# A mixture-of-experts layer whose experts are ranked on the chip, with fixed row counts per rank and column-tiled up-projections

## The reference

```
grp = argmax(x @ group_w + b)                    # top-1 of 4 groups
top2 = the two largest of the 8 expert logits in that group
gate = softmax(top2 logits) * softmax(group logits)[grp]
for each of 32 experts e, over the rows routed to it:
    h = silu(xb @ w1[e]) * (xb @ w3[e])          # 1024 -> 512, twice
    y += gate * (h @ w2[e])                      # 512 -> 1024
```

## Time and profile before

| | |
|---|---|
| median of 3 runs | 1710.05 us (1709.49 to 1710.27) |
| the profiled execution | 1708.72 us, of which the span is 1707.1 |
| TensorE busy | 1592.7 us, 93% |
| VectorE, ScalarE, GpSimd busy | 537.5, 396.1, 167.6 us |
| up-matmuls (L1703) | x1088, 480.1 us |
| down-matmuls (L1727) | x544, 240.9 us |
| the chain that ended last | TensorE 91% of the span |
| HBM read, written | 301.42 MB, 66.06 MB |

### The profile page before, as it was taken

How to read it: one execution, slowest core, us unless ns; L and a number is a source line. 1 busy time by engine, 2 the same in 40 slices (tenths; PEclk the granted TensorE clock), 3 DMA queues, 4 the chain that set the end, 5 groups by cost and what they waited for, 6 DMA issues and landing times.

```text
span 1707.1 us, 20384 instructions
## 1 busy us (share of the span) xinstructions
PE 1592.7 (93%) x7532; PEld 795.0 (47%) x7532; DVE 537.5 (31%) x1115; ACT 396.1 (23%) x578; POOL 167.6 (10%) x230
## 2 busy tenths in 40 slices
PE   7999999999999988998948999999999999999990
PEld 3444455546545545554524444444444444444440
DVE  4840064345536426353572111111111111111114
ACT  4020154354355343123411000000000000000004
POOL 2010000000000000100011111111011111111100
PEclk9999999999999998999967999999999999999995
DMA  5132132142132333335938788888889988898848
GB/s 216 50 113 74 66 130 80 45 142 88 50 104 77 112 136 127 135 119 198 336 125 356 263 336 336 332 332 334 336 339 344 343 332 333 332 332 334 332 157 307
DMA packets 76851, 368.43 MB, mean 216 GB/s; under 512 B 9072, under 2 KB 21872, under 8 KB 63600
## 3 DMA queue, kind: packets, MB, share of 16 engines
q1 hardware_dynamic: 57488, 300.90, 46.0%
q0 software_dynamic: 18720, 65.02, 12.4%
q10 hardware_dynamic: 576, 1.59, 0.2%
HBM read 301.42 MB, written 66.06 MB: 215 GB/s over the span
## 4 chain that ended last, share of the span: by engine, by line
PE 91%; DVE 3%; DMA 2%; issue 2%; ACT 2%; DVEq 0%; ACTq 0%; SPq 0%; POOLq 0%
PE bank L1703 28%; PE bank L1441 24%; PE bank L1727 14%; PE bank L1572 7%; PE bank L1453 5%; PE bank L1614 2%; PE bank L1696 2%; PE bank L1531 2%; PE bank L1548 1%; PE bank L1547 1%; PE bank L1526 1%; PE bank L1718 1%; PE bank L1632 1%; PE bank L1626 1%; PE bank L1483 1%
## 5 line engine op out<-in xcount | busy, mean ns | idle before, releaser
L1703 PE MATMUL bank<-wup,xgT 128*128 128x512 f32 x1088 | 480.1, 594 | 1.4 <-ACT xgT L935 1.4
L1441 PE MATMUL bank<-wide,mid 128*128 128x512 f32 x960 | 417.4, 594 | 2.6 <-issue 2.6
L1703 PEld LDWEIGHTS bank<-wup,xgT 128*128 128x128 f32 x1088 | 204.5, 191 | 246.2 <-issue 244.1
L1441 PEld LDWEIGHTS bank<-wide,mid 128*128 128x128 f32 x960 | 182.0, 191 | 227.7 <-issue 227.5
L1727 PE MATMUL bank<-wide,hidT 128*128 128x512 f32 x544 | 240.9, 596 | 4.2 <-DVE hidT L1411 4.2
L1727 PEld LDWEIGHTS bank<-wide,hidT 128*128 128x128 f32 x544 | 101.3, 191 | 119.3 <-issue 119.3
L1572 PE MATMUL bank<-early,mid 128*128 128x512 f32 x288 | 124.8, 592 | 0.0
L942 ACT ACTIVATE sil<-bank 128x512 f32<-128x512 f32 x34 | 20.3, 597 | 434.5 <-PE bank L1703 434.5
L1384 DVE TENSOR_SCALAR mid<-bank,gate_of 128x512 f32<-128x512 f32 x68 | 51.0, 751 | 212.3 <-PE bank L1727 212.3
L731 POOL DMA_INDIRECT x_dram<-mid,sidx x34 | 53.6, 1577 | 644.0 <-DVE mid L1384 297.3
L935 ACT ACTIVATE xgT<-bank 128x512 f32<-128x512 f32 x70 | 38.1, 594 | 275.1 <-PE bank L1696 275.1
(11 more groups left out here) (214 smaller groups left out, 1327.3 us busy)
## 6 DMA issues: line engine op xcount, KB each, us to landing
wup<-w SPq DMA_DIRECT2D x68, 2048.0 KB, 17.9
wide<-w SPq DMA_DIRECT2D x34, 2048.0 KB, 9.5
u_dram<-ustage POOLq DMA_DIRECT2D x60, 256.0 KB, 2.4
rin<-u_dram SPq DMA_DIRECT2D x60, 256.0 KB, 4.3
mid<-w_in SPq DMA_DIRECT2D x23, 512.0 KB, 3.4
wide<-x_t SPq DMA_DIRECT2D x12, 512.0 KB, 11.3
mix_dram<-mixst POOLq DMA_DIRECT2D x24, 256.0 KB, 2.6
mid<-x_all SPq DMA_DIRECT2D x12, 512.0 KB, 5.5
```

What stands on the lines that cost most here:

```text
L1441: last = pe.matmul(PROJ[u % 3][:, :], wsec[:, slot, k, :], nT[:, k, g * GT:(g + 1) * GT], start=(k == 0), stop=(k == KT - 1))
L1703: last = pe.matmul(bank[out_bank][:, :], xgT[:, k, :], weights[:, s, k, :], start=(k == 0), stop=(k == KT - 1))
```

## The change

Experts are ranked by their count, ties by number. Rank r has block r, whose number of rows is fixed: 128 for ranks 0 to 3, 112 for 4 to 15, 104 for 16 to 31. What an expert has beyond its capacity goes to extra blocks from number 32 on, up to 32 of them. The up products are turned round: 32 columns of the weights are the stationary operand in each of four column tiles, and the transposed rows move past them, so an instruction moves 104, 112 or 128 columns and not 512. The hidden values then come out transposed, and `transpose_hidden` and `copy_hidT` go; `hidT` has two buffers. [...] The count product of TensorE gives its result by expert and tile, so that one scan makes the running sums.

```diff
+CAPACITY = ((0, 128), (4, 112), (16, 104))
+MAIN_BLOCKS = NE
+MAX_OVER = -(-(2 * T // (CAPACITY[-1][1] + 1)) // EIGHT) * EIGHT
+BLOCK_COLUMNS = MAIN_BLOCKS + MAX_OVER + 2
@@ blocks_loop
-            pairs = (MIN_BLOCKS - first) // 2
-            with eng.Fori(0, pairs) as i:
-                for j in range(2):
-                    body(2 * i + (first + j), (first + j) % 2)
-            rest = first + 2 * pairs
-            with eng.Fori(0, -(-(MAX_BLOCKS - rest) // EIGHT)) as k:
+            if first % 2:
+                body(first, first % 2)
+                first += 1
+            ends = [b for b, rows in CAPACITY if b > first] + [MAIN_BLOCKS]
+            for start, end in zip([first] + ends[:-1], ends):
+                with eng.Fori(0, (end - start) // 2) as i:
+                    for j in range(2):
+                        body(2 * i + (start + j), (start + j) % 2, capacity(start))
+            rest = MAIN_BLOCKS
+            with eng.Fori(0, MAX_OVER // EIGHT) as k:
                 with eng.If(k * EIGHT + rest < used):
                     with eng.Fori(0, EIGHT // 2) as i:
                         for j in range(2):
                             with eng.If(k * EIGHT + 2 * i + (rest + j) < used):
...
@@ routing, VectorE
-            link(dve.memset(offset[:, 0, :], 0.0))
-            for t in range(NT):
-                link(dve.tensor_tensor(offset[:, t + 1, :], totals[:, t, :], offset[:, t, :], ALU.add))
+            link(dve.tensor_tensor_scan(upto[:, :, :].rearrange("p e t -> p (e t)"),
+                                        first_tile[:, :, :].rearrange("p e t -> p (e t)"),
+                                        bank[1][:, 0:NT * NE], 0.0, ALU.mult, ALU.add))
+            link(dve.tensor_tensor(above[:, :, :], counted[:, :].unsqueeze(1).to_broadcast([P, NE, NE]),
+                                   counted[:, :].unsqueeze(2).to_broadcast([P, NE, NE]), ALU.is_gt))
+            link(dve.tensor_reduce(rank[:, :], above[:, :, :], axis=AX.X, op=ALU.add))
...
+            link(dve.tensor_tensor(masked[:, :, :], slots[:, :, :], by_expert(cap), ALU.is_ge))
+            link(dve.tensor_tensor(masked[:, :, :], masked[:, :, :], by_expert(to_over), ALU.mult))
...
@@ blocks, VectorE
+                dve.tensor_tensor(hidT[:, s, :, :].rearrange("p k c -> p (k c)"), sil[:, :], bank[3][:, :],
+                                  ALU.mult).then_inc(hid_ready, 1)
@@ blocks, GpSimd
-            blocks_loop(pool, 3, used, rows_in_and_out)
+            for b in range(3, MAIN_BLOCKS):
+                rows_in_and_out(b, b % 2)
...
@@ blocks, TensorE
-                for k in range(KT):
-                    last = pe.matmul(bank[out_bank][:, :], xgT[:, k, :], weights[:, s, k, :],
-                                     start=(k == 0), stop=(k == KT - 1))
+                for f in range(FT):
+                    for k in range(KT):
+                        for c0 in range(0, P, SUB):
+                            last = pe.matmul(bank[out_bank][c0:c0 + SUB, f * P:f * P + rows],
+                                             weights[:, s, k, f * P + c0:f * P + c0 + SUB], xgT[:, k, 0:rows],
+                                             start=(k == 0), stop=(k == KT - 1), tile_position=(0, c0))
...
-            def expert_step(b, s):
-                first_up(b, s)
-                transpose_hidden(b - 1)
-                second_up(b, s)
+            def expert_step(b, s, rows=P):
+                first_up(b, s, rows)
+                second_up(b, s, rows)
                 transpose_rows(b + 1, 1 - s)
                 down(b - 1, 1 - s)
```

More of the change, by code:

```diff
@@ L53, with capacity @@
 FT = FE // P
-MAX_BLOCKS = (2 * T + NE * (P - 1)) // P
-MIN_BLOCKS = 2 * T // P
+CAPACITY = ((0, 128), (4, 112), (16, 104))
+MAIN_BLOCKS = NE
 EIGHT = 8
-BLOCK_COLUMNS = MAX_BLOCKS + 2
+MAX_OVER = -(-(2 * T // (CAPACITY[-1][1] + 1)) // EIGHT) * EIGHT
+BLOCK_COLUMNS = MAIN_BLOCKS + MAX_OVER + 2
+def capacity(b):
+    if not isinstance(b, int) or b >= MAIN_BLOCKS:
+        return P
+    return [rows for first, rows in CAPACITY if first <= b][-1]
 C_MIX, C_SCALE, C_GAIN, C_LB = 0, KT, KT + POOLS, KT + POOLS + 1
@@ L435, in blocks_loop @@
                             with eng.If(k * EIGHT + 2 * i + (rest + j) < used):
-                                body(k * EIGHT + 2 * i + (rest + j), (first + j) % 2)
+                                body(k * EIGHT + 2 * i + (rest + j), (rest + j) % 2)
         block = always.enter_context(nc.Block())
@@ L560, in _, with load_expert @@
             sp.wait_ge(blocks_known, 1)
-            used = sp.value_load(blocks_over[0:1, 0:1], min_val=0, max_val=MAX_BLOCKS - MIN_BLOCKS) + MIN_BLOCKS
-            def load_expert(b, s):
+            used = sp.value_load(blocks_over[0:1, 0:1], min_val=0, max_val=MAX_OVER) + MAIN_BLOCKS
+            def load_expert(b, s, rows=P):
+                first = isinstance(b, int) and b < 2
                 e = sp.value_load(expert_of[0:1, ds(b, 1)], min_val=0, max_val=NE - 1)
-                if not isinstance(b, int):
+                if not first:
                     sp.wait_ge(h1_ready, b - 1)
@@ L702, in _ @@
                       allow_small_or_imprecise_dtypes=True)
-            pool.affine_select(out=before[:, :], in_=ones[:, :], compare_op=ALU.is_gt, fill=0.0,
-                               base=0, pattern=[[1, P]], channel_multiplier=-1).then_inc(ranks_ready, 1)
+            pool.iota(expert_id[:, :], pattern=[[1, NE]], base=0, channel_multiplier=0,
+                      allow_small_or_imprecise_dtypes=True)
+            pool.memset(before[:, :], -1.0).then_inc(before_filled, 1)
+            pool.memset(first_tile[:, :, :], 1.0).then_inc(before_filled, 1)
+            pool.wait_ge(before_filled, 2)
+            pool.memset(first_tile[:, :, 0:1], 0.0)
+            pool.affine_select(out=before[:, :], in_=before[:, :], compare_op=ALU.is_ge, fill=0.0,
+                               base=0, pattern=[[-1, P]], channel_multiplier=1).then_inc(ranks_ready, 1)
             pool.wait_ge(parts_ready, 1)
@@ L744, in rows_in_and_out @@
                 add_outputs(b - 1, 1 - s)
-            blocks_loop(pool, 3, used, rows_in_and_out)
+            for b in range(3, MAIN_BLOCKS):
+                rows_in_and_out(b, b % 2)
+            with pool.Fori(0, MAX_OVER // EIGHT) as k:
+                with pool.If(k * EIGHT + MAIN_BLOCKS < used):
+                    with pool.Fori(0, EIGHT // 2) as i:
+                        for j in range(2):
+                            with pool.If(k * EIGHT + 2 * i + (MAIN_BLOCKS + j) < used):
+                                rows_in_and_out(k * EIGHT + 2 * i + (MAIN_BLOCKS + j), j)
             for s in range(2):
@@ L1746, in _ @@
             blocks_loop(pe, 3, used, expert_step)
-            transpose_hidden(used - 1)
             for s in range(2):
```

116 lines of the change are left out of this document (64 added, 52 removed).

## The result

| | before | after |
|---|---|---|
| median | 1709.89 us (1709.49 to 1710.27, 4 runs) | 2026.97 us (2022.74 to 2030.49, 4 runs) |
| ratio, 95% interval | 1 | 1.1852 (1.1837 to 1.1867) |
| span of the profiled execution | 1707.1 us | 2026.5 us |

What follows compares the result with a forecast made beforehand. TensorE was taken as the bound, DMA close behind. The profiled 1708.7 us plus 139 for the stage, 15 for the ladder and 4 for routing gave 1867, with 1.3 for the median 1868 us; range 1662 to 1985, the forecast's own 1780 to 1950.

Steps and rivals of the forecast that it cites:

- rival A: Up-matmuls: the queue fetches ahead and hides instruction fetch, if a packet's turn is under 2.9 us; 1666 us; chance 0.2.
- the place and the mechanism: Up-matmuls: TensorE idles for instructions, about 3 gaps of 2 us a block, busy share near 0.75.
- The array: TensorE with 32-column tiles, not limited by fetch: 19.4, 20.3 or 22.0 us a block for 104, 112 or 128 rows.
- the turn L: Instruction queue in the expert blocks: time per packet, taken as 5.0 us; forecast's span 4.2 to 5.8 us.
- The block's formula: Expert block's period: 10.0 us plus 3.2 packet turns.
- the ladder: Skipped extra blocks after the last one run: jumps that miss cost +15 us, bounds 0 and +40.
- rival B: Instruction queue: a packet's turn is 6 us and more, as under full weight traffic; 1987 us; chance 0.15.
- rival C: Expert stage: the clock falls and lengthens the down-matmuls by 2.3 us a block; +78 us, 1946 us; chance 0.13.
- Routing +4: Routing on VectorE, for which TensorE waits: added scan, compare and reduces cost +4 us, bounds +2 and +7.
- Branches back at nothing: Loop's end: the branch back costs nothing, covered by 6.9 us of queued down-matmuls; 44 us without that cover.

Runs made afterwards that it cites:

- e1: Changed kernel with one 128-column weight load in place of four 32-column ones in the up products; 1713.6 us, 1.0016 of the time before.
- e2: Changed kernel with two column tiles of 64 columns in place of four of 32; 1656.5 us, 0.9682 of the time before.
- e6: Form with two 64-column tiles, TensorE's fixed-count loops taking four blocks a pass in place of two; 1678.5 us, 0.9816 of the time before.
- e9: Changed kernel with four added 512-column matmuls a block in the up products; 2053.5 us, 1.1997 of the time before.
- e11: Form with two 64-column tiles plus four added 512-column matmuls a block; 1817.9 us, one run.
- e7: Changed kernel with the first up product in 32-column tiles and the second in 64-column tiles; 1759.6 us, 1.0288 of the time before.
- e13_half: Changed kernel, each expert weight transfer bringing half of its bytes from the third block on; 1896.1 us, one run.
- e4_caps128: Changed kernel with every block at 128 rows in place of 104, 112 and 128; 2011.2 us, one run.
- e10: Changed kernel with eight added 512-column matmuls a block in the up products; 2084.9 us, 1.2177 of the time before.
- e12: Changed kernel with room for 8 extra blocks in place of 32, so no skipped groups; 2014.1 us, one run.
- e3_light: Changed kernel, each expert weight transfer bringing a sixteenth of its bytes from the third block on; 1787.1 us, one run.

## Why the prediction was wrong
**What the prediction says of the instruction stream, by the traces.** A program matmul is two matmuls and two weight loads in both forms: the kernel before has 1088 of each at L1703, for 34 blocks of 16, and the changed kernel 17408 of each at L1761, for 34 blocks of 256. They come 256 or so to a packet (127 and 127 for one). The heads' loop is fetched anew: its second pass, 483.4 to 625.4 us, runs some 1860 instructions and has nine packets. The packet after a jump is asked for at once: the branch back begins at 483.29 us, one packet comes between 484 and 485, the next between 487 and 488, and none between 488 and 512. From the first to the second TensorE ran two matmuls and two weight loads (the packets in the windows 484 to 485, 487 to 488 and 483.4 to 625.4, then TensorE's busy time in the window 484.3 to 487.4):

```profile
q8 instruction: 1, 0.02, 5.9%
...
q8 instruction: 1, 0.02, 5.7%
...
q8 instruction: 9, 0.15, 0.4%
...
484.30:487.40 3.10, 0.48 (x2) 0.47 (x2) 0.00 (x0) 3.06 (x4) 0.51 (x1) 0.89 0.25 90
```
So the second packet was asked for up to some 250 instructions before it was needed (an estimate from the 256 of a packet). And before the change TensorE's idle time put down to issue is the 2.6 us after this branch and the 1.98 us of the earlier trace rows, and no more. The trace thus bears rival A out in both of its points, that the queue fetches ahead and that no straight stretch but one ran dry. Neither shows that a fast stream is covered, and the 98 stalls of the changed kernel show that it isn't.

**Right: the place and the mechanism.** The sign, the gaps marked issue, about three in each block (98 in 34), the row counts that no longer matter, TensorE's busy share (0.75) and roughly the DMA share (0.66; 0.75 was said) and the packets (163 more; 143 were said) came as forecast. e1, e2 and e6 show that it is the number of instructions together with a body that isn't kept, e9 and e11 that TensorE has room to spare.

**The array: right for tiles of 64, not for those of 32.** 19.4, 20.3 and 22.0 us per block are what e2_tile64 has (19.5, 20.3, 22.0), but they were worked out for tiles of 32, at 91, 98 and 111 ns for a group of four. No run shows these terms, nor the 2.9 us for a packet of up-matmuls that follows from the first. The kernel before has 429 ns for an instruction of 512 columns (6.87 us for 16), 56.7 ns for a group of four tiles of 57 columns (96 in 1.36 us) and at most 48 ns for one of 36; a group of 104 rows took 112 ns in e7's kept loop (7.1 to 7.2 us for 64), and a packet of 112-row matmuls 3.27 us in the changed kernel. e7's kept loop has 1.4 us more for each 32-column product. Rival A's sum of 1666 us is 10 us from e2's time; that is luck, since it was meant for the form with tiles of 32, which at e7's rate would save nothing (an estimate: 22.3 us for a 104-row block against 21.9 before) even with the fetch hidden.

**The step that failed: the turn L, 5.0 us.** The prediction had four readings, 3.4, 4.0, 6.1 and 7.6 us, and named the last two as those under full weight traffic. It then took 5.0, because "steps that get longer leave the weights' queue emptier". The DMA engines did get emptier, a share of 0.66 against 0.89, but the turn stayed at 6.85 us. e13_half shows why that argument gives so little: at a share of 0.47 most turns are still the long ones, and the mean is 5.6 us. At a sixteenth of the bytes the turn is 4.0. The block's formula was roughly sound: 10.0 + 3.2 x 6.85 is 31.9 us, against 31.2 measured (its first term had grown by 0.6 us through the clock, see below, so it is a good 1 us too high). By it the 31.2 us mean an L of 6.6, and 3.2 x 1.6 x 34 = 174 us is what the step is short of, against the 159 us between forecast and result; the ladder, taken 11 us too high, makes up most of the rest. The readings of the place that was at stake should have been used, and not a mean with readings from quiet places: rival B (L = 6.1, 1987 us) was the nearest case, with a chance of 0.15, and still 40 us short.

**Right in sight, wrong in size: the clock (rival C, +78 us).** Before the change it was at 1.00 in the stage and at 0.50 for the 3.3 us after the 2.6 us of idle at 484. It did fall: 198 us of the 32 periods were at the lower level. But it cost less. Where there are no gaps for it to hide in, in the down products and the transposes, the changed kernel took 10 us more each than e2, some 20 us in all; the changed kernel's rows of them, and e2's:

```profile
L1779 PE MATMUL bank<-wide,hidT 128*128 128x512 f32 x544 | 249.3, 612 | 8.9 <-issue 8.9
L1752 PE MATMUL bank<-ident,mid 128*128 128x128 f32 x280 | 49.2, 333 | 2.0 <-DMA mid<-xn_dram,gidx 2.0
```
```profile
L1779 PE MATMUL bank<-wide,hidT 128*128 128x512 f32 x544 | 239.2, 592 | 1.0 <-DVE mid L1442 1.0
L1752 PE MATMUL bank<-ident,mid 128*128 128x128 f32 x280 | 39.1, 284 | 0.6 <-DMA mid<-xn_dram,gidx 0.6
```
These 20 us are part of the 317; e4_caps128, with half of the low clock, got 15 us of them back and was 16 us faster. In the up products there is time for the low clock: e10 brings the clock to 0.99 and the turn isn't shorter. By the slope between blocks in one trace (0.5 us of period for each us at the low level) I would have put 100 us down to it; blocks with longer stalls have more low clock, and the slope shows only this.

**The small terms.** Routing +4: measured 4.9 on TensorE. Ladder +15 with bounds 0 and +40: 6.4 by e12, with the spread told there, and against the kernel before, which has a ladder of its own, the last period grew by 4.0. Not in the sum at all: the first blocks, 12.6 us between the first up product and the first down product, which are straight-line code; the trace has five stalls put down to issue in them, 9.9 us in all. No run changes these blocks alone. Branches back at nothing: 153 packets in 32 periods are 4.8 a block where the body's length gives 4.2, so a pass fetches a packet or so more than it has; what that costs by itself was not measured.

Where the 317 us are: the 32 periods 298, the first blocks 12.6, routing 4.9, the last period 4.0, together with roundings the 319.4 us between the spans of the two profiled executions.

## What to carry to other kernels
Before splitting a matmul into column tiles, count the loop body's instructions and the time in which 256 of them pass; if the body is longer than what stays on the engine (here between 1140 and 1860) and 256 instructions pass in less than a packet's turn (3.3 us against 6.85 here), expect the stage to run at that turn, as it did here; it is to be read where the big transfers run. Choose the coarsest tile that still lets the array follow the rows: 64 columns gave a gain of 3.2% here, and 32 turned it into a loss of 18.5%. And to tell a starved engine from a busy one, give it more work: 9.4 us of matmuls a block cost 1.7.

## What the runs showed of the hardware that was not expected
- With 128 weight columns the step is 112 ns for 104 moving rows as for 128 (e1_full, all periods 22.0 us), while 64-column tiles side by side follow the rows (20.3 and 19.5 us).
- With no packet coming, a product of 32-column tiles still took 7.1 to 7.2 us where one of 64-column tiles took 5.9, with two pauses of 0.3 us in it (e7_mixed).
- A body of 1650 instructions was kept on every pass in one loop and fetched on every second in another of the same kernel (e7_mixed).
- The granted clock of the stage was 1.00 in e3_light, whose 124 stalls in the 32 periods are 0.6 us on average (1.78 and 0.96 us in the block shown), and 0.91 in the changed kernel, whose stalls are 2.6 us on average.
- The DMA engines moved 359 GB/s with a share of 1.01 when no fetch held the stage (e2_tile64); before it was 335 at 0.89.
